# First root of a two-block kernel taken token by token from the rows of x instead of channel by channel from the turned x

## The reference, cut to what matters

```python
def rmsnorm(x, g):
    xf = x.astype(jnp.float32)
    y = xf * lax.rsqrt(jnp.mean(xf * xf, axis=-1, keepdims=True) + EPS)
    return (y * g.astype(jnp.float32)).astype(x.dtype)

def modulate(h, shift, scale):
    return h * (1 + scale) + shift

# first_block, mixer kind 0
mod_lat = split(silu(c) @ ada_w[i] + ada_b[i], 6)
a_lat = modulate(rmsnorm(h_lat, g_pre), mod_lat[0], mod_lat[1])
b_gate, c_gate, v = split(a_lat @ w_in, 3)        # then a short convolution, gates, w_out
h_lat = h_lat + mod_lat[2] * rmsnorm(y_lat, g_post)
h_lat = h_lat + mod_lat[5] * rmsnorm(squared_relu_mlp(modulate(rmsnorm(h_lat, g_pre_ff), ...)), g_post_ff)
# second_block: attention and pooling, a convolution block, and two feed-forwards
```

## Time and profile before

| | us |
|---|---|
| median of 3 runs | 1722.91 (1722.45 to 1723.51) |
| the profiled execution, device time | 1723.58 |
| its span, first to last instruction | 1721.8 |
| PE busy | 1697.1 |
| DVE busy | 1096.6 |
| ACT busy | 699.0 |
| POOL busy | 159.3 |

### The profile page before, as it was taken

One profiled execution on the slowest core, in us unless ns is written; L12 is line 12 of the kernel. 1 busy time (PEld: TensorE's weight loads), 2 busy tenths in 40 slices (PEclk: granted clock), 3 DMA queues, 4 the chain that ended last, 5 costly groups with the idle time before them and its releaser, 6 DMA issues.

```text
span 1721.8 us, 21514 instructions
## 1 busy us (share of the span) xinstructions
PE 1697.1 (99%) x7685; PEld 1374.9 (80%) x7685; DVE 1096.6 (64%) x1663; ACT 699.0 (41%) x1021; POOL 159.3 (9%) x145
## 2 busy tenths in 40 slices
PE   8999999999999999999999999999999999999999
PEld 7888868888888789788888888877656888888888
DVE  6799885353534685645663663669998666366364
ACT  4322353232323345844432432446676443243242
POOL 1000400000000040000000000005892000000000
PEclk9999999999999999999999999999999999999999
DMA  9576314323333132002222222232210323223222
GB/s 295 178 243 221 125 57 137 98 98 98 116 98 98 49 99 93 31 26 98 98 98 98 97 98 89 81 99 74 74 49 28 120 97 99 85 94 112 75 85 86
DMA packets 182338, 176.22 MB, mean 102 GB/s; under 512 B 3304, under 2 KB 181740, under 8 KB 182268
## 3 DMA queue, kind: packets, MB, share of 16 engines
q1 hardware_dynamic: 182268, 175.29, 31.8%
HBM read 173.15 MB, written 2.10 MB: 102 GB/s over the span
## 4 chain that ended last, share of the span: by engine, by line
PE 87%; DVE 5%; POOL 4%; issue 2%; ACT 1%; DMA 1%; POOLq 0%; SPq 0%; DVEq 0%; ACTq 0%
PE PSUM L1582 23%; PE PSUM L1583 23%; PE PSUM L1584 23%; POOL CP L537 3%; DVE PSUM L1514 1%; PE PSUM L1947 1%; PE PSUM L1945 1%; PE PSUM L1946 1%; PE PSUM L1920 1%; PE PSUM L1900 1%; PE PSUM L1672 1%; PE PSUM L1614 1%; PE PSUM L1616 1%; PE PSUM L1979 1%; PE PSUM L1980 1%
## 5 line engine op out<-in xcount | busy, mean ns | idle before, releaser
L577 ACT ACTIVATE WH<-RAW 128x1024 fp32r<-128x1024 f32 x274 | 281.5, 1052 | 726.6 <-PE PSUM L1584 684.5
L1582 PE MATMUL PSUM<-XH,WH 128*128 128x512 f32 x1152 | 449.5, 390 | 0.0
L1583 PE MATMUL PSUM<-XL,WH 128*128 128x512 f32 x1152 | 448.2, 389 | 0.0
L1584 PE MATMUL PSUM<-XH,WL 128*128 128x512 f32 x1152 | 448.2, 389 | 0.0
L977 DVE TENSOR_TENSOR WL<-RAW,WH 128x1024 fp32r<-128x1024 f32 x274 | 343.6, 1276 | 8.1 <-ACT WH L577 8.0
L1582 PEld LDWEIGHTS PSUM<-XH,WH 128*128 128x128 f32 x1152 | 216.3, 188 | 45.7 <-issue 0.7
L1583 PEld LDWEIGHTS PSUM<-XL,WH 128*128 128x128 f32 x1152 | 216.3, 188 | 45.4 <-issue 0.7
L1584 PEld LDWEIGHTS PSUM<-XH,WL 128*128 128x128 f32 x1152 | 216.3, 188 | 44.8
L1582 PE MATMUL PSUM<-HH,WH 128*128 128x512 f32 x644 | 251.3, 390 | 0.4
L1584 PE MATMUL PSUM<-HH,WL 128*128 128x512 f32 x644 | 250.6, 389 | 0.0
L1583 PE MATMUL PSUM<-HL,WH 128*128 128x512 f32 x644 | 250.6, 389 | 0.0
(11 more groups left out here) (347 smaller groups left out, 2000.7 us busy)
## 6 DMA issues: line engine op xcount, KB each, us to landing
RAW<-in_ffn_w_up SPq DMA_DIRECT2D x44, 1024.0 KB, 5.0
ARAW<-in_ada_w SPq DMA_DIRECT2D x24, 1024.0 KB, 5.3
RAW<-in_mlp_w_in SPq DMA_DIRECT2D x16, 1024.0 KB, 5.3
RAW<-in_mlp_w_out SPq DMA_DIRECT2D x16, 1024.0 KB, 4.9
RAW<-in_ffn_w_down SPq DMA_DIRECT2D x16, 1024.0 KB, 5.1
RAW<-in_sc_w_in SPq DMA_DIRECT2D x9, 1024.0 KB, 5.2
RAW<-in_even_w_in SPq DMA_DIRECT2D x8, 1024.0 KB, 5.6
RAW<-in_odd_w_pw SPq DMA_DIRECT2D x16, 512.0 KB, 4.7
```

The costliest lines, as they stand in the source:

```text
L577: act.activation(WH[:, j, a:b, :], RAW[:, j, a:b, :], ACT.Copy).then_inc(s_hi, 1)
L1582: pe.matmul(o, wh, mh[:, k, :], start=(k == 0), stop=False)
L1583: pe.matmul(o, wh, ml[:, k, :], start=False, stop=False)
L1584: mm = pe.matmul(o, wl, mh[:, k, :], start=False, stop=(k == kn - 1))
```

## The change

The root of the first norm is formed from XROW. x comes in four DMAs, one for each 128 tokens, in the same place of the queue. ACT squares each block of rows and sums it along the channels in the same instruction (`accum_out`), takes Ln and Exp of four numbers a partition, and puts the roots on four diagonals. PE multiplies a matrix of ones with these (`first_root`), so ST_BANK now holds the root itself for each token, and DVE reads it there. The squares' additions on POOL and DVE, two matmuls and Ln and Exp of 512 columns are gone. With it the order of the first step is written anew: PE turns x by blocks of tokens, runs 34 instead of 26 fillers first, and waits for all eight copies of x ahead of its next filler; each chunk 0 and 1 has its own scale, shift and split order; unit 2 of pieces 0 and `first_lo(0)` come later; `mod_unit(5)` comes ahead of XL of chunk 1; two SP waits have other counters.

Since ST_BANK holds a root, ACT takes Ln and Exp(-2 ln) of it around unit 11, and the sum at ST_X1 multiplies it by D in a scalar_tensor_tensor, where a tensor_tensor stood.

```diff
@@ SP
-                    sp.wait_ge(s_xt, DC)
-                elif i >= 2:
-                    sp.wait_ge((s_ad, s_ap)[part], i - 1)
+                    sp.wait_ge(s_xt, 2 * TB)
+                    sp.wait_ge(s_xq, TB)
+                elif i == 2:
+                    sp.wait_ge((s_ac, s_ap)[part], 1)
+                elif i == 3:
+                    sp.wait_ge((s_ad, s_ap)[part], 2)
...
-            sp.dma_start(XROW[:, :, :], x_rows).then_inc(s_xin, 16)
+            for b in range(TB):
+                sp.dma_start(XROW[:, b, :], i["x"][0, b * P:b * P + P, :]).then_inc(s_xin[b], 16)
@@ ACT
+            def root_of_rows():
+
+                for b in range(TB):
+                    act.wait_ge(s_xin[b], 16)
+                    act.activation(MACC[:, (2 + b) * D:(3 + b) * D], XROW[:, b, :], ACT.Square,
+                                   accum_out=sc_(S_RS + b)).then_inc(s_xq, 1)
...
+                for b in range(TB):
+                    act.activation(TF[:, 1, b * P:b * P + P], IDENT[:, :].bitcast(F32), ACT.Copy, scale=sc_(S_RR + b)
+                                   ).then_inc(s_dg, 1)
...
-            for c in range(DC):
-                act.wait_ge(s_xu, c + 1)
-                act.activation(first_square(c), X[:, c, :], ACT.Square).then_inc(s_sqr, 1)
-            first_hi(0)
-            act.wait_ge(s_const, 1)
-            rms(ST_X0, 1.0 / D)
-            for i in range(4):
+            root_of_rows()
+            first_hi(0, (0, 1))
+            act.wait_ge(s_sm, 3)
+            split_shift(0, S_GS0, S_MOD, (0,))
+            first_hi(0, (2,))
+            act.wait_ge(s_sm, 4)
+            split_shift(0, S_GS0, S_MOD, (1,))
+            first_hi(1)
+            for i in range(1, 4):
...
+            act.activation(PS_[:, S0_BANK, :], PS_[:, S0_BANK, :], ACT.Ln).then_inc(s_ms, 1)
+            act.wait_ge(s_ms, 1)
+            act.activation(PS_[:, S0_BANK, :], PS_[:, S0_BANK, :], ACT.Exp, scale=-2.0).then_inc(s_ms, 1)
@@ DVE
-                tt(TA[:, c % 2, :], X[:, c, :], R[:, :], ALU.mult).then_inc(sp_t, 1)
+                tt(TA[:, c % 2, :], X[:, c, :], PS_[:, ST_BANK, :], ALU.mult).then_inc(sp_t, 1)
...
+            dve.wait_ge(s_xu, 8)
+            dve.wait_ge(s_ss, ST_X0 + 1)
+            scaled_x(0)
+            scaled_x(1)
+            dve.wait_ge(s_ac, 1)
...
+            gs.then_inc(s_sm, 1)
+            first_lo(0, (0, 1))
+            dve.wait_ge(s_ap0, 1)
+            tt(sc_(S_MOD), PS_[:, COL_BANK, 0:1], col("ada_b", 0), ALU.add).then_inc(s_sm, 1)
+            x_lo(0)
+            first_lo(0, (2,))
+            dve.wait_ge(s_ap, 1)
+            tt(sc_(S_MOD + 1), PS_[:, SHIFT_BANK, 1:2], col("ada_b", 1), ALU.add).then_inc(s_sm, 1)
+            mod_unit(5)
+            x_lo(1)
+            scaled_x(2)
+            scaled_x(3)
+            first_lo(1)
...
-            tt(v, PS_[:, S0_BANK, :], v, ALU.add).then_inc(s_ss, 1)
+            dve.wait_ge(s_ms, 2)
+            stt(v, PS_[:, S0_BANK, :], float(D), v, ALU.mult, ALU.add).then_inc(s_ss, 1)
@@ PE
+            def first_root():
+
+                pe.wait_ge(s_dg, TB)
+                for b in range(TB):
+                    mm = pe.matmul(PS_[:, ST_BANK, b * P:b * P + P], ONES[:, :], TF[:, 1, b * P:b * P + P],
+                                   start=True, stop=True)
+                mm.then_inc(s_ss, 1)
...
-            for _ in range(26):
+            for _ in range(34):
...
             pe.wait_ge(s_ve, 1)
-            scale_columns(0)
-            shift_products(0, 0, 4)
+            pe.wait_ge(s_xu, 8)
             keep_busy_on_x()
...
+            shift_products(0, 0, 2)
+            first_root()
+            shift_products(0, 2, 12)
             keep_busy_on_x()
...
+            first_chunk_of_x(0)
+            shift_products(0, 12, 16)
+            first_chunk_of_x(1)
+            pe.wait_ge(s_sm, 4)
+            first_chunk_of_x(2)
+            shift_products(1, 0, 8)
+            pe.wait_ge(s_x, 2)
+            first_product(0, 1)
+            shift_products(1, 8, 16)
+            first_product(1, 1)
+            scale_columns(1)
+            first_product(2, 1)
+            for i in range(1, 4):
+                pe.wait_ge(s_x, 2 * i + 1)
```

More of the change, by code:

```diff
@@ L228, in program @@
         s_hi, s_lo = sem("half_unit_hi"), sem("half_unit_lo")
-        s_raw0 = [sem(f"first_pieces_loaded_{i}") for i in range(4)]
+        s_raw0 = [None] + [sem(f"first_pieces_loaded_{i}") for i in range(1, 4)]
         s_hi0, s_lo0 = sem("first_piece_hi"), sem("first_piece_lo")
@@ L679, in _ @@
             act.wait_ge(s_ss, ST_X1 + 1)
-            act.activation(SQ[:, :], TF[:, 0, :], ACT.Ln, bias=sc_(S_EPS), scale=1.0 / D).then_inc(s_ln, 1)
+            act.activation(SQ[:, :], TF[:, 0, :], ACT.Ln, scale=1.0 / D).then_inc(s_ln, 1)
             act.wait_ge(s_ln, ST_X1 + 1)
@@ L993, in banks, with mod_unit @@
                 return PS_[:, 2 * j + c, :]
-            def mod_unit(a):
+            def mod_unit(a, c0=0):
                 i = a - 4
@@ L1107, in scaled_x, with x_lo, copy_x, first_lo @@
             def scaled_x(c):
-                tt(TA[:, c % 2, :], X[:, c, :], R[:, :], ALU.mult).then_inc(sp_t, 1)
-            def first_lo(i):
-                for u in range(FIRST):
+                tt(TA[:, c % 2, :], X[:, c, :], PS_[:, ST_BANK, :], ALU.mult).then_inc(sp_t, 1)
+            def x_lo(c):
+                dve.wait_ge(sp_h, c + 1)
+                tt(XL[:, c, :], TF[:, c % 2, :], XH[:, c, :].bitcast(F32), ALU.subtract).then_inc(s_x, 1)
+            def copy_x(b):
+                for h in range(2):
+                    step = 2 * b + h
+                    dve.wait_ge(s_xt, step + 1)
+                    dve.tensor_copy(X[:, 4 * h:4 * h + 4, b * P:b * P + P],
+                                    PS_[:, step % 4, :].rearrange("p (c t) -> p c t", c=4)).then_inc(s_xu, 1)
+            def first_lo(i, units=range(FIRST)):
+                for u in units:
                     raw, hi, lo = first_unit(u, i)
@@ L1747, in _ @@
-            keep_busy_on_x()
-            keep_busy_on_x()
-            for i in range(4):
-                if i:
-                    pe.wait_ge(s_x, 2 * i + 1)
-                if i < 3:
-                    if i == 0:
-                        first_chunk_of_x()
-                    else:
-                        for u in range(FIRST):
-                            pe.wait_ge(s_lo0, pieces(i, u))
-                            first_product(u, 2 * i)
-                            shift_products(i + 1, (0, 6, 11)[u], (6, 11, 16)[u])
+            pe.wait_ge(s_ad, 1)
@@ new lines, in _ @@
+            for n in range(2):
+                mm = pe.matmul(PS_[:, SCALE_BANK, 8 + n:9 + n], MACC[:, (8 + n) * P:(9 + n) * P], ONES[:, 0:1],
+                               start=True, stop=True)
+            mm.then_inc(s_ac, 1)
+            shift_products(0, 0, 2)
+            first_root()
+            shift_products(0, 2, 12)
+            keep_busy_on_x()
+            first_chunk_of_x(0)
+            shift_products(0, 12, 16)
+            first_chunk_of_x(1)
+            pe.wait_ge(s_sm, 4)
@@ new lines, in _ @@
+            first_chunk_of_x(2)
[6 more added lines that the diff above has]
+            first_product(2, 1)
+            for i in range(1, 4):
+                pe.wait_ge(s_x, 2 * i + 1)
+                if i < 3:
+                    for u in range(FIRST):
+                        pe.wait_ge(s_lo0, pieces(i, u))
+                        first_product(u, 2 * i)
+                        shift_products(i + 1, (0, 6, 11)[u], (6, 11, 16)[u])
```

119 lines of the change are left out of this document (56 added, 63 removed).

## The result

The changed kernel is slower: median 1729.95 us (1729.27 to 1732.10, 6 runs) against 1723.18 us, ratio 1.0041 with a 95% interval of 1.0030 to 1.0052. The forecast was 1725.2 us in 1722.2 to 1727.2: the time lies outside the range. One execution of e13, at 2872 us where its others took 1725 to 1732, enters no figure here.

The account below looks back on a forecast made before the run. PE, busy for 99% of the span, was taken as the bound. Start of step 1 +1.2, half clock +1.0 and the second norm's sum +0.06 gave +2.3 us: 1725.2 us, range 1722.2 to 1727.2 (8 in 10).

Parts of the forecast that it names:

- x, copies, root: From x's arrival to the root: transposes at 13.1 to 13.25 us, copies 13.8 to 18.7, root 21.5, gaining 2.5 us.
- Step 1's first wait: PE's wait for XL ahead of step 1: step 1 can begin at 41.4 us against 40.2, kept as +1.2 us.
- Root to XH: DVE and ACT from the root to chunk 0's XH: 26.1 us against 26.66, leaving 0.6 of 2.5 us gained.
- The gain of 1.8 us at this point: At the first products: PE's fillers no longer hold them, so they begin at 26.15 us instead of 27.95.
- Step 0: From the first products at 26.15 us: XL of chunk 1 at 33.35, queued behind mod_unit(5); scale_columns(1) done at 38.5.
- Both stalls: PE's new waits for XL: 0.4 us inside step 0 for chunk 1, and 1.4 us ahead of step 1.
- The clock: Half clock when the first products begin, with 2 us left of such a spell: +1.0 us.
- SP, second norm: Nothing waits for SP's loads; Ln and Exp at the second norm are hidden; DVE's sum there adds 0.06 us.
- Rival 2: Half clock lasts through the first three units of the products: +3.8 us, 1726.7 us; chance 0.16.
- Rival 1: Full clock for the products, step 1 can begin at 41.4 us: +1.26 us, 1724.2 us; chance 0.20.
- Rival 3: The early root carries through without the two stalls, step 1 can begin at 38.5 us: 1721.2 us; chance 0.10.
- Rival 4: Transposes do nothing for the clock: half from about 18.7 us, products at 28.3, +4.5 us, 1727.4 us; chance 0.06.

Follow-up runs that it names:

- e13: e7 with three 512-column fillers instead of one ahead of the first products; 1725.37 us, 1.0023 of the kernel before.
- e10: The changed kernel with three 512-column fillers instead of one directly ahead of the first products; 1729.59 us, 1.0030 of the kernel before.
- e4: The kernel before with its old root and only the new order inside step 0; 1724.34 us, 1.0008 of the kernel before.
- e14: e10 with XL of chunk 1 ahead of mod_unit(5), step 1's 16 shift products together and scale_columns(1) ahead of chunk 1's units; 1726.56 us, 1.0022.
- e7: The changed kernel's start, with the old order from the root on and one filler ahead of the products; 1735.44 us, 1.0052 of the kernel before.
- e9: The kernel before with one instead of two 512-column fillers between its last shift products and first products; 1729.22 us, 1.0030.
- e1: The changed kernel with eight more identity fillers in PE's idle ahead of the last copies of x; 1729.23 us, 1.0032 of the kernel before.
- e8: e3 with its three fillers spread among step 0's shift products, so that one, not two, stands last; 1730.07 us, 1.0027 of the kernel before.
- e12: e3 with all 16 shift products of step 0 right behind the root, then three fillers in a row; 1721.18 us, 0.9985 of the kernel before.
- e3: The changed kernel's new root with the kernel before's order behind it, 26 starting fillers and three 512-column fillers ahead of the products; 1721.28 us, 0.9986.
- e11: e3 with all 16 shift products of step 0 right behind the root, then two fillers in a row; 1721.22 us, 0.9984 of the kernel before.
- e2: e1 with two more 512-column fillers between the root and the first products; 1727.61 us, 1.0024 of the kernel before.

## Why the prediction was wrong

- **x, copies, root.** Right. Transposes were forecast at 13.1 and came at 13.08; copies 13.8 and 18.7, measured 13.55 and 18.44. The split copies cost 4.88 us as before. The squares on ACT take 1.06 us and 0.19 for the sum, the diagonals are ready at 16.0: off the path. (The five terms under "Step 1's first wait" add up to +1.2, not to the +1.0 that stands there; +1.2 is what was kept.)
- **Root to XH.** The order of the steps was right, the time 0.9 late: `first_root` took 1.92 us for eight passes, not 0.9, since the clock was at half from about 20.3 us. XH came at 26.96 instead of 26.1. The products came at 28.39 instead of 26.15: the 20 shift passes took 4.06 us and the filler 1.92, and "by about 25.9 at half" was too early by 2.5 us, 0.9 of it the later root. The gain of 1.8 us at this point became a loss of 0.4.
- **Step 0.** Both stalls were named rightly, as the execution of e10 without half clock shows: the wait for XL of chunk 1 ends at 34.36 with DVE queued behind `mod_unit(5)`, though PE waited there for 0.1 us only, not 0.4; the wait ahead of step 1 took 1.5 us (1.4 forecast), and the whole step 15.10 us against 15.25. e4 gives the same price for the order, 1.7 us, on the old root.
- **The clock.** This is the step that failed: "I expect the clock at half when the products begin", 1.0 us. That it would be at half was right. Its price in the profiled execution (the slowest of the six) is 48.0 - 41.4 = 6.6 us; by median the whole forecast was 4.75 us short. 2.2 us of the 6.6 were lost before the first product, 4.4 behind it, where I had allowed 1.0. I had taken the length of the spell from the one row of before, 24.4 to 27.4 us, as if a spell had a length of its own, and had no second one. In the profiles here a spell of the first 60 us lasts from 3.4 us (e14) to 31 (e7). That of before lay over four filler passes; e9 shows the kernel before without the second filler at 1729.2 us. I had written that these fillers "held PE until 27.95" and counted their going as a gain, and had priced half clock too low for one-column passes, which cost twice as much too (3.21 us for 16 against 1.68 in e10).
- **SP, second norm.** The shift weights of step 2 were issued at about 31 us, behind the wait that was named, and PE waited for none of it. The scalar_tensor_tensor took 0.69 us, no more than the tensor_tensor. The 0.7 us lost there lie in a half-clock spell (about 235 to 242 us), and there is one near that place in other kernels' profiles too (e1, e10, e13, e14).
- **The rivals.** Rival 2 had the sign and came nearest in mechanism, but 3.8 us for one spell through three units is not what happened: the first spell ended with the first unit, and a second lay over chunk 1. Its counter-argument, "no longer spell" in the row, was the same error. Rival 1 describes step 0 as e10 caught it, but that is another kernel: none of the changed kernel's six executions lies under 1729.2 us. Rival 3 was out. Rival 4 forecast the start of the products best, 28.3 us against 28.39. Its clock was to be at half from about 18.7, and was at 1.00 until about 20.3, filler included. Whether transposes keep the clock up no run here tells: none changes them alone.

What stays open: what lets a spell begin in one execution and not in another of the same kernel, and how many wide matmuls end it (chance may have a part: e7, e8 and e9 have executions 9 to 12 us apart); why three fillers suffice for e12 and, in six of nine executions, not for e10; and how much of the upper group belongs to the changed kernel's start. No upper execution of e10 or e13 was profiled.

## What to carry to other kernels

A filler that seems to stand in the way may be what keeps PE's clock up behind it: before it is removed, or spread, look at the granted clock of the stretch that follows, not at busy time, and try wide matmuls in one row directly ahead of the real work (two in a row helped e3, against e8, and the kernel before, against e9; three weren't enough for e10). When one spell of half clock is seen, ask what ended it, and price the case in which that is gone. Split a change of order from a change of algorithm: here the new root gained 2 us, and the order written around it, with the clock that it brought, lost nearly 9.

## What the runs showed of the hardware

- A busy PE is not enough for full clock: e7 had PE busy for 30.38 of 30.60 us at 1.2 GHz, and 14.7 us of that were six matmuls of 512 columns in turn with 12 or 10 one-column passes. The same stream runs at 2.4 GHz in e11, where it is entered at that level. And in e2 the clock fell at about 25 us with PE busy for 4.00 of 4.00 us before it.
- At 1.2 GHz a one-column pass takes 0.20 us in a row and at 2.4 GHz 0.105 (3.21 and 1.68 us for 16), so half clock costs small matmuls nearly as much, in proportion, as wide ones.
- An ACT pass of 1024 columns with a sum along them adds a second instruction of 0.19 us to 1.06.
- The first microseconds vary too, and the granted clock doesn't show it. The 34 fillers at the very start end at 13.08 us in the profile of the changed kernel and at 14.18 in that of e10, with 1.00 in both. But a pass lasts 421 ns until about 6.5 us in the one and until about 8.9 in the other, and 275 ns from there on: that is where the 1.1 us went. Where the column is silent, the duration of a known pass tells.
